# Second block with tokens on the partitions where a norm follows: one core, fp32 split into high and low parts

## What is computed

```python
def _layer_norm(x, g, b):
    mu = x.mean(-1, keepdims=True)
    var = jnp.square(x - mu).mean(-1, keepdims=True)
    return (x - mu) * lax.rsqrt(var + NORM_EPS) * g + b

for l in range(DEPTH):                       # second_block
    proj = x @ w_in[l]                       # r_q, r_k, r_v, r_g, m_qk, m_v, m_o, gates
    ...                                      # retention and mLSTM, gated and projected
    mix = (gate_a * y_ret + gate_b * y_ml) @ w_out[l]
    x = _layer_norm(DEEPNORM_ALPHA * x + mix, ln1_g[l], ln1_b[l])
    ff = (silu(x @ w_gate) * (x @ w_up)) @ w_down[l]
    x = _layer_norm(DEEPNORM_ALPHA * x + ff, ln2_g[l], ln2_b[l])
```

## Time and profile before

| | before |
|---|---|
| median of the runs | 2140.08 us |
| the profiled execution's own time | 2141.11 us |
| its span | 2139.3 us |
| PE, DVE, ACT busy | 97%, 60%, 48% |
| mean granted TensorE clock | 0.990 |

### The profile page before, as it was taken

How to read it: one execution, slowest core, us unless ns; L and a number is a source line. 1 busy time by engine, 2 the same in 40 slices (tenths; PEclk the granted TensorE clock), 3 DMA queues, 4 the chain that set the end, 5 groups by cost and what they waited for, 6 DMA issues and landing times.

```text
span 2139.3 us, 39735 instructions
## 1 busy us (share of the span) xinstructions
PE 2072.3 (97%) x16726; PEld 2017.7 (94%) x16748; DVE 1277.7 (60%) x1144; ACT 1030.1 (48%) x975; POOL 120.3 (6%) x83
## 2 busy tenths in 40 slices
PE   7999999999999998899999999999998999999997
PEld 6999998999999997699999999999998999999996
DVE  6556655655665667456557556755445666665445
ACT  5445645534443366344436454544345563545343
POOL 4000000100100002020000001010001000001001
PEclk9999999999999999899999999999999999999999
DMA  6555443455465544035545344435553443554452
GB/s 252 198 192 177 166 170 118 162 193 190 163 217 182 191 163 155 37 139 206 195 176 197 138 158 158 178 123 212 180 192 120 159 162 136 187 186 158 177 194 80
DMA packets 51562, 360.32 MB, mean 168 GB/s; under 512 B 5632, under 2 KB 7808, under 8 KB 8320
## 3 DMA queue, kind: packets, MB, share of 16 engines
q1 hardware_dynamic: 50768, 355.18, 45.8%
q0 software_dynamic: 688, 3.60, 0.5%
HBM read 357.71 MB, written 1.05 MB: 168 GB/s over the span
## 4 chain that ended last, share of the span: by engine, by line
PE 92%; DVE 4%; ACT 2%; issue 1%; POOL 0%; DMA 0%; ACTq 0%; SPq 0%; DVEq 0%; POOLq 0%
PE ps L236 25%; PE ps L237 25%; PE ps L238 25%; PE ps L283 2%; PE ps L285 2%; PE ps L284 2%; PE ps L272 1%; DVE wlo L232 1%; PE ps L267 1%; PE ps L268 1%; PE ps L585 1%; ACT whi L227 1%; PE ps L1486 1%; PE ps L1478 1%; DVE in_lo L440 1%
## 5 line engine op out<-in xcount | busy, mean ns | idle before, releaser
L232 DVE TENSOR_TENSOR wlo<-raw,whi 128x2048 fp32r<-128x2048 f32 x335 | 783.0, 2339 | 520.0 <-ACT whi L227 519.0
L236 PE MATMUL ps<-in_hi,whi 128*128 128x256 f32 x3708 | 1050.5, 283 | 10.8 <-DVE wlo L232 4.9
L237 PE MATMUL ps<-in_lo,whi 128*128 128x256 f32 x3708 | 1039.2, 280 | 0.0
L238 PE MATMUL ps<-in_hi,wlo 128*128 128x256 f32 x3708 | 1038.5, 280 | 0.0
L227 ACT ACTIVATE whi<-raw 128x2048 fp32r<-128x2048 f32 x335 | 638.4, 1908 | 238.3 <-PE ps L238 214.0
L236 PEld LDWEIGHTS ps<-in_hi,whi 128*128 128x128 f32 x3708 | 701.9, 189 | 18.6 <-issue 5.3
L237 PEld LDWEIGHTS ps<-in_lo,whi 128*128 128x128 f32 x3708 | 702.3, 189 | 2.1 <-issue 1.4
L238 PEld LDWEIGHTS ps<-in_hi,wlo 128*128 128x128 f32 x3708 | 701.9, 189 | 0.0
L236 PE MATMUL ps<-h_hi,whi 128*128 128x256 f32 x960 | 270.9, 282 | 0.0
L237 PE MATMUL ps<-h_lo,whi 128*128 128x256 f32 x960 | 269.8, 281 | 0.0
L238 PE MATMUL ps<-h_hi,wlo 128*128 128x256 f32 x960 | 269.4, 281 | 0.0
(11 more groups left out here) (251 smaller groups left out, 1728.9 us busy)
## 6 DMA issues: line engine op xcount, KB each, us to landing
raw<-in_slots SPq DMA_DIRECT2D x335, 1024.0 KB, 4.8
ws<-in_mem_t POOLq DMA_DIRECT2D x2, 1024.0 KB, 8.5
consts<-in_consts SPq DMA_DIRECT2D x1, 1600.0 KB, 13.2
consts<-in_consts POOLq DMA_DIRECT2D x1, 1472.0 KB, 6.7
x<-in_x_t SPq DMA_DIRECT2D x1, 1024.0 KB, 7.6
y_t<-x SPq DMA_DIRECT2D x1, 640.0 KB, 3.4
y_t<-x SPq DMA_DIRECT2D x1, 384.0 KB, 3.7
params<-in_params SPq DMA_DIRECT2D x1, 105.0 KB, 14.5
```

The lines of the kernel that those rows point to most:

```text
L232: dve.tensor_tensor(wlo[:, j], raw[:, j], whi[:, j].bitcast(F32), ALU.subtract).then_inc(lo_ready, 1)
L236: pe.matmul(out, whi[:, j, o:o + n], hi, start=start, stop=False, skip_group_check=True)
L237: pe.matmul(out, whi[:, j, o:o + n], lo, start=False, stop=False, skip_group_check=True)
L238: return pe.matmul(out, wlo[:, j, o:o + n], hi, start=False, stop=stop, skip_group_check=True)
```

## The change

It has these parts, all in the second block and in the FFN before it:

- The last projection before a norm (`w_out` slots, and all down slots of the last three FFNs) is multiplied with the activations as the stationary side: its result is tokens by features. A down slot is `pe_down_part` for two halves of the tokens (t) and two halves of the features (h), 24 matmuls with 512 columns of weights.
- x is kept as tokens by features (`x_tok`, two halves of 128 tokens). It is turned once, by 16 transposes in the last FFN of the first block (L547 of the new kernel), and copied back by ScalarE. The result y is stored without a turn, in three transfers.
- The norm runs along the free axis on VectorE: add, `bn_stats`, `bn_aggr`, subtract mean and multiply with the gain, multiply with 1/std and add the bias; ScalarE only takes Ln and Exp of one column. Gains and biases come as 128 equal rows by DMA (1 MB for each norm, two issues by GpSimd in each layer).
- For the next product each half is turned by 8 transposes (`pe_turn_y`) into PSUM, from which ScalarE and VectorE write `in_hi` and `in_lo`.
- The order goes by halves of the tokens: the first half of a norm's input is finished before the second, and the transposes stand inside the matmuls of the second half and of the next pair.
- The first two slots after a norm lie in an own buffer (`first_w`) instead of the ring. Their product is tokens by features; the first two slots of a layer are therefore now values (`S_RV0`), and FFN group 0 is turned back by 4 transposes (L557). The later mLSTM row product (`aT`) moves behind one slot and the retention's values.
- The layer loop is written out twice; the copy of parameters `lp` and two dummy slots at the end go.

```diff
+        x_tok = x[:, :, :].rearrange("p a b -> p (a b)").rearrange("p (t h n) -> p t h n", t=2, h=2)
...
+        def act_first_hi(act, c, u):
+            j = c % RING
+            act.wait_ge(raw_full[j], 16 * (c // RING + 1))
+            act.activation(first_hi(u), raw[:, j], ACT.Copy).then_inc(hi_ready, 1)
...
+        def turn_bank(m, t, h):
+            return ps[:, 4 + h if m % 2 else 2 * t + h, :]
+        def pe_turn_y(pe, m, t):
+            for h in range(2):
+                pe.wait_ge(y_done, 4 * m + 2 * t + h + 1)
+                for k in range(4):
+                    last = pe.transpose(turn_bank(m, t, h)[:, k * P:(k + 1) * P], x_tok[:, t, h, k * P:(k + 1) * P], ident)
+                last.then_inc(y_turned, 1)
+        def act_tok_hi(act, m, t):
+            for h in range(2):
+                act.wait_ge(y_turned, 4 * m + 2 * t + h + 1)
+                src = turn_bank(m, t, h).rearrange("p (a b) -> p a b", a=4)
+                act.activation(in_hi[:, 4 * h:4 * h + 4, t * P:(t + 1) * P], src, ACT.Copy).then_inc(tok_hi, 1)
+        def dve_tok_lo(dve, m, t):
+            for h in range(2):
+                k, a = slice(4 * h, 4 * h + 4), slice(t * P, (t + 1) * P)
+                src = turn_bank(m, t, h).rearrange("p (a b) -> p a b", a=4)
+                dve.wait_ge(tok_hi, 4 * m + 2 * t + h + 1)
+                dve.tensor_tensor(in_lo[:, k, a], src, in_hi[:, k, a].bitcast(F32), ALU.subtract).then_inc(tok_lo, 1)
...
+        def pe_tok_half(pe, out, w_hi, w_lo, t, m=None, pause=None, then=None):
+            a, o = slice(t * P, (t + 1) * P), out[:, t * 256:(t + 1) * 256]
+            for g in range(2):
+                if m is not None:
+                    pe.wait_ge(tok_hi, 4 * m + 2 * t + g + 1)
+                for k in range(4 * g, 4 * g + 4):
+                    if k == pause:
+                        then()
+                    w = slice(k * 256, k * 256 + 256)
+                    pe.matmul(o, in_hi[:, k, a], w_hi[:, w], start=(k == 0), stop=False, skip_group_check=True)
+                    pe.matmul(o, in_hi[:, k, a], w_lo[:, w], start=False, stop=False, skip_group_check=True)
+                if m is not None:
+                    pe.wait_ge(tok_lo, 4 * m + 2 * t + g + 1)
+                for k in range(4 * g, 4 * g + 4):
+                    w = slice(k * 256, k * 256 + 256)
+                    last = pe.matmul(o, in_lo[:, k, a], w_hi[:, w], start=False, stop=(k == DT - 1), skip_group_check=True)
+            return last
+        def pe_first_pair(pe, outs, m):
+            w = [(first_hi(u), first_lo(u)) for u in range(2)]
+            pe_tok_half(pe, outs[0], *w[0], 0, m)
+            pe_tok_half(pe, outs[1], *w[1], 0, None, 6, lambda: pe_turn_y(pe, m, 1))
+            pe_tok_half(pe, outs[0], *w[0], 1, m).then_inc(slot_used, 1)
+            pe_tok_half(pe, outs[1], *w[1], 1).then_inc(slot_used, 1)
...
+        def pe_down_part(pe, j, hi, lo, t, h, first=False):
+            o, a = ps[:, 2 * t + h, :], slice(t * P, (t + 1) * P)
+            for kk in range(2):
+                w = slice(kk * D + h * 512, kk * D + h * 512 + 512)
+                pe.matmul(o, hi[:, kk, a], whi[:, j, w], start=(first and kk == 0), stop=False, skip_group_check=True)
+                pe.matmul(o, hi[:, kk, a], wlo[:, j, w], start=False, stop=False, skip_group_check=True)
+                last = pe.matmul(o, lo[:, kk, a], whi[:, j, w], start=False, stop=False, skip_group_check=True)
+            return last
...
+                pe.wait_ge(fin_log, f + 1)
+                for t in range(2):
+                    for k in range(DT):
+                        last = pe.transpose(ps[:, 2 * t + k // 4, (k % 4) * P:(k % 4 + 1) * P], x[:, k, t * P:(t + 1) * P], ident)
+                last.then_inc(x_turned, 1)
+                up(0, 3, 0)
...
+                pe_first_pair(pe, (gate0_ps, up0_ps), m_in)
+                gate(0, 2, 0)
+                pe.wait_ge(ffn_mul, fb + 1)
+                for kk in range(2):
+                    for t in range(2):
+                        last = pe.transpose(ps[:, 3, kk * T + t * P:kk * T + (t + 1) * P],
+                                            hidden[:, t * 256 + kk * P:t * 256 + (kk + 1) * P], ident)
+                last.then_inc(h_turned, 1)
+                up(0, 3, 0)
+            down(0, 4, 0, True)
...
+            for h in range(2):
+                pe_down_part(pe, s9 % RING, h_hi, h_lo, 0, h)
+            pe.wait_ge(lo_ready, s10 + 1)
+            pe.wait_ge(ffn_hl, fb + LASTF + 1)
+            for h in range(2):
+                pe_down_part(pe, s10 % RING, last_hi, last_lo, 0, h).then_inc(down_half, 1)
+            for h in range(2):
+                last = pe_down_part(pe, s9 % RING, h_hi, h_lo, 1, h)
+            last.then_inc(slot_used, 1)
+            pe_down_part(pe, s10 % RING, last_hi, last_lo, 1, 0).then_inc(down_half, 1)
+            if m_out is not None:
+                pe_turn_y(pe, m_out, 0)
+            pe_down_part(pe, s10 % RING, last_hi, last_lo, 1, 1).then_inc(slot_used, 1)
...
+        gains = [view(6144, 2, 2, 512), view(8192, 2, 2, 512)]
+        def out_bank(i, t):
+            return i - 2 if i >= 2 and t else i
+        def dve_ln_add(dve, l, i, v, new, t, part):
+            dve.scalar_tensor_tensor(v, v, DEEP_ALPHA, new, ALU.mult, ALU.add).then_inc(ln_sum, 1)
+            dve.wait_ge(ln_sum, LN_SUMS * l + i)
+            dve.bn_stats(ln_parts6[:, t, 6 * part:6 * part + 6], v).then_inc(ln_stats, 1)
+        def act_ln_rstd(act, l, which, t):
+            q, r = 4 * l + 2 * which + t, ln_r[:, t:t + 1]
+            act.wait_ge(ln_mean, q + 1)
+            act.activation(r, ln_mv[:, t, 1:2], ACT.Ln, bias=eps[:, 1:2]).then_inc(ln_log, 1)
+            act.wait_ge(ln_log, q + 1)
+            act.activation(r, r, ACT.Exp, scale=-0.5).then_inc(ln_rstd, 1)
+        def dve_ln_tok(dve, l, which, t, stats, parts):
+            q = 4 * l + 2 * which + t
+            dve.wait_ge(ln_stats, LN_SUMS * l + stats)
+            dve.bn_aggr(ln_mv[:, t], ln_parts6[:, t, 0:6 * parts]).then_inc(ln_mean, 1)
+            dve.wait_ge(ln_mean, q + 1)
+            dve.wait_ge(gb_loaded[which], 16 * (l + 1))
+            g, b = gains[which][:, 0], gains[which][:, 1]
+            for h in range(2):
+                v = x_tok[:, t, h]
+                dve.scalar_tensor_tensor(v, v, ln_mv[:, t, 0:1], g[:, h], ALU.subtract, ALU.mult).then_inc(ln_centred, 1)
+            dve.wait_ge(ln_rstd, q + 1)
+            for h in range(2):
+                v = x_tok[:, t, h]
+                dve.wait_ge(ln_centred, 2 * q + h + 1)
+                dve.scalar_tensor_tensor(v, v, ln_r[:, t:t + 1], b[:, h], ALU.mult, ALU.add).then_inc(y_done, 1)
...
+        def dve_entry(dve, t, h):
+            wait_down(dve, 3, t, h)
+            dve.wait_ge(x_tok_set, 1)
+            v = x_tok[:, t, h]
+            dve.scalar_tensor_tensor(v, ps[:, 2 * t + h, :], 0.5, v, ALU.mult, ALU.add).then_inc(y_done, 1)
+        def dve_ln2_add(dve, l, t, h):
+            wait_down(dve, l + 4, t, h)
+            dve_ln_add(dve, l, 9 + 2 * t + h, x_tok[:, t, h], ps[:, 2 * t + h, :], t, h)
...
-            for i in proj(B2_OUT, 0, range(DT), parts({0: 7, 2: 8, 4: 9, 6: 10})):
-                if i:
-                    pe_ln_mean(pe, n, i - 1)
-            pe_ln_mean(pe, n, 3)
-            pe_ln_var(pe, n)
-            pe_ffn(pe, l + 4, B2_FFN, r3, ln_parts(pe, n + 1))
-            for i in range(4):
-                pe_ln_mean(pe, n + 1, i)
-            pe_ln_var(pe, n + 1)
+            c = B2_OUT + 3 * r3
+            ready = parts({0: 7, 2: 8, 4: 9, 6: 10})
+            pe.wait_ge(lo_ready, c + 1)
+            pe.matmul(ps[:, 0, :], zeros[:, 0:P], zeros[:, :], start=True, stop=False, skip_group_check=True)
...
+            out_tile(1, 0)
+            out_tile(1, 1).then_inc(slot_used, 1)
+            out_tile(2, 0).then_inc(out_half, 1)
+            out_tile(3, 0).then_inc(out_half, 1)
+            pe.wait_ge(ln_sum, LN_SUMS * l + 4)
+            out_tile(2, 1).then_inc(slot_used, 1)
+            out_tile(3, 1, 4, lambda: pe_turn_y(pe, 2 * l + 1, 0)).then_inc(slot_used, 1)
+            pe_ffn_tok(pe, l + 4, B2_FFN + 3 * r3, 2 * l + 1, 2 * l + 2 if l < LAYERS - 1 else None)
...
-            for s in range(4):
-                act_hi(act, B2_OUT + s + 2, r3)
-            act_ln_factor(act, n)
-            act_ln_parts(act, n, "ln1_b")
-            act_ln_shift(act, n, "ln1_b")
+            act_hi(act, B2_OUT + 2, r3)
+            act_hi(act, B2_OUT + 3, r3)
+            act_first_hi(act, B2_FFN + 3 * r3, 0)
+            act_first_hi(act, B2_FFN + 1 + 3 * r3, 1)
+            act_log_exp(act)
+            act_ln_rstd(act, l, 0, 0)
+            act_tok_hi(act, 2 * l + 1, 0)
+            act_hi(act, B2_FFN + 2, r3)
+            act_ln_rstd(act, l, 0, 1)
+            act_tok_hi(act, 2 * l + 1, 1)
             act_ffn(act, l + 4, B2_FFN, r3, False)
-            act_ln_factor(act, n + 1)
```

(80 more changed lines are left out.)

316 lines of the change are left out of this document (166 added, 150 removed).

## The result

The changed kernel took 2088.81 us, the median of four runs (2084.97 to 2089.54), against 2140.93 us (2138.69 to 2144.73) for the one before: ratio 0.9752, 95% interval 0.974 to 0.9763. The forecast was 2082. Three further times, on other occasions, it had 2084.71, 2088.55 and 2085.20. The profiled execution had an own time of 2088.40 us and a span of 2086.6, so 52.7 us less than the profiled one before, where the sum said 57.7.

A forecast was written before the change was run, and what follows sets the result against it. TensorE was taken to bound the kernel (busy 97%, 92% of the chain of waits). Terms 16.3 + 12.5 + 13.3 - 2.5 + 15.5 + 2.6 = 57.7 us off 2141.1, less 1.0 for the median: 2082 us, range 2073 to 2102.

The forecast's parts named there:

- the down slots: 33 slots in three FFNs: 24 matmuls of 512 columns at 0.217 us replace 48 narrow ones, 0.47 us each, 15.5 gained.
- wide matmuls bring nothing: Rival for the 512-column down matmuls: the extra 0.01 us goes with the columns, 15.5 us missing, 2098 us; chance 0.12.
- no other slot changed: Sign to look for: down slots of the last three FFNs at 5.2 us, all other slots as before.
- Norm 1: Between output projection and FFN, twice: sums and waiting go, 2.7 us cost remains, 8.2 gained per layer, 16.3 us.
- Norm 2: Between the second block's layers: 18.3 us of sums, waiting and half clock become 5.8 us, 12.5 gained.
- The end: From PE's last matmul to the end of the kernel: 22.9 us become 9.6, 13.3 us gained.
- Between the blocks: Where the first block hands to the second: 32 added transposes, 3.9 us, make a loss of 2.5 us.
- Clearing: Clearing of four banks in three FFNs goes, 12 at 0.217 us, 2.6 us gained.
- Layer 1's body: Layer 1 up to its output projection: no change, 0 us; the clock's fall inside it was taken to stay.
- no falls in the layers: Rival: two half-clock stretches inside the layers, 6.9 and 3.4 us, vanish; 5 us more gained, 2077 us; chance 0.08.
- The rival of late halves and clock: At three norms PE waits for DVE in pieces, half clock follows each: 15 us lost, 2097 us; chance 0.12.

The follow-up runs named there:

- the written-out kernel: The kernel before the change with only its second-block layer loop written out on three engines: 2135.07 us against 2139.67, ratio 0.9977.
- the narrow one: The changed kernel with each 512-column down matmul written as two of 256 columns: 2089.41 us against 2084.71 for the changed kernel.
- the one without halves: The changed kernel with the first token half's norm put behind the second half's sums: 2106.40 us, 21.7 more than the changed kernel.
- that program: A separate small program streaming independent matmuls of each format and width plus 160 transposes, only TensorE at work; 512-column fp32r took 0.227 us each.
- the split products: The changed kernel with the four fp32 selection-matrix products issued in two places of two, one slot apart: 2099.79 us against 2088.55.

## Why the prediction was right, and where it was not

The sign and the size held: the time fell within the range, 7 us above the forecast (5.0 in the profiled spans; the rest is mostly the 1.0 us taken off for the median, which this time lay 0.4 above the profiled run). The mechanism held at the norms and at the end. It did not at the down slots, the second largest term, and part of the closeness is luck.

**The step that failed is the down slots**: "I take 0.217: 5.68 - 5.21 = 0.47 us a slot, 15.5 us." The wide matmul is 0.2333 in the kernel, the slot 5.60, the gain 0.07 to 0.08 us a slot, 2.4 us. 13 us of the forecast are missing, and the rival "wide matmuls bring nothing" is the one that came true, with its 0.236. Even the 0.08 need not be the width's, since the untouched narrow slots of the first block gained as much; that also misses the forecast's "no other slot changed". The inference from fp32 to fp32r was the fault. Two fp32 records of 256 columns cost nearly what one of 512 does (0.216 and 0.429), so that row spoke for a cost that goes with the columns, and so for no gain; instead its price, which has 2 to 3 ns over the columns, was given to a format that by itself has 13 to 14, and in this kernel even those went with the columns. Even the form by itself (0.1200 and 0.2267) would have given only 0.32 us a slot. The Trainium skill ("TensorE: Matmul & The Clock Gate", Back-to-back issue gap) has N / 2.4 + 2.5 ns. Bf16 agrees (0.109 at 256), fp32r does not: 0.1167 and 0.2333 in the kernel, 0.120 and 0.227 by itself. Its estimate of the saving, 2 us, came out near the measured one through two errors that cancel.

**Why the time was still only 7 us off.** Other terms were too small by 8 us in all. Some 3 us of that hang together with the miss, since longer down slots cover more of DVE's work; that the others went the same way is luck.

- Norm 1 (16.3 us for two): 9.1 us went between the output projection and the FFN in each layer; less 0.4 for the hidden group's transposes, 17.5 in all. There is no waiting, where 0.3 us were written for each, and a transpose is 0.87 / 8 = 0.11 us, not 0.12.
- Norm 2 (12.5 us): 15.4 us went there and behind it; less 0.9 for the 8 transposes that stand in FFN 4's stage, 14.5. VectorE came as counted: from the last hidden part (1596.36) to the first y (1603.66) 7.3 us, where the count has 7.7. But PE's waits are 1.6 us and not 3.9 (none ahead of the first transposes, where 1.4 were counted), since PE arrives later: half a down slot takes 2.8 us and not 2.6, and covers DVE. Part of what the down slots did not give came back here. Some 5 us of this term are the loop's end, as the forecast said of the 3.4 us for the third slot and of the clock; the written-out kernel shows it.
- The end (13.3 us): 15.5. From the last pass of DVE (2083.43) to the end of the span are 3.2 us, where 4.1 were taken as a bound; and PE's last matmul is 0.8 us later than counted (four halves of a slot at 0.2 each), so less is left behind it.
- Between the blocks (loss 2.5): 1.9. The table's 0.8, and 1.7 that down slots and clearing gave in that stage, less 0.6 for a low part that is no longer late, which falls into layer 1.
- Clearing (2.6): 0.86 us in each FFN, as said.
- Layer 1's body, nothing in the sum: those 0.6 us, and a fall of the clock that is 3.4 us long and not 6.8, 1.7 us. The fall itself stayed, so the rival "no falls in the layers" did not come true. In layer 1 it is 3.4 us long in all four profiles of the changed kernel, and 6.8 in the kernel before, its written-out form, the narrow one and the one without halves; what sets the length no run shows.

**The rival of late halves and clock** had its premise in waits of DVE. It didn't happen since the halves hide them; the kernel without halves shows what it would have been, and more: 21.7 us, with the clock at half behind each of the three norms. It also had the rule of the Trainium skill on its side ("TensorE: Matmul & The Clock Gate", PE-mode transpose), that transposes do not count as activity. The row of 160 transposes, 17.5 us with no other work on PE, does not bear it out. Windows of that program, transposes first, then the fp32r row behind them:

```profile
185.99:203.46 17.47, 17.47 (x163) 1.00 0.00 1
203.46:214.99 11.53, 11.51 (x96) 1.00 0.01 1
```

The clock stayed at 1.00 through them and after, and so it did at the turned halves of the kernel. What the clock fell behind in the second block was waiting (norm 2 before, the three norms without halves, the slots behind the split products), and products with 4 rows in use. Waiting alone doesn't make it sure: at norm 1 of the kernel before PE stood still for 3.1 of 27 us, and the clock stayed at 1.00.

## What to carry to other kernels

When a term of the sum multiplies a small difference by many instructions, measure the form at its new size by itself before trusting it, and take it only from rows of the same number format: 16 ns on each of 792 matmuls was the largest error here. A norm between two rows of matmuls hides in halves of the tokens: the second half's matmuls cover the first half's norm, and where waiting on TensorE is followed by half the clock, as it was here behind waits of 3.7 to 4.3 us at the norms without halves, a microsecond of waiting removed is worth more than itself. Before crediting a restructuring, write out the loop alone: here 4.6 us of a gain of 51 to 55 us needed nothing else. And look at slots that weren't touched: if their price moved too, a part of the gain belongs to something else.

## What the runs showed that was not expected

- An fp32r matmul costs N / 2.4 plus 13 to 14 ns by itself (0.1205, 0.173, 0.227 us for 256, 384, 512 columns), an fp32 record twice N / 2.4 plus 2 to 3. In the FFN of the changed kernel it is 0.4557 ns a column instead (0.1167, 0.2333). The cause of the difference is open.
- The same 48 fp32r matmuls of a down slot took 5.68 us in the kernel before and 5.60 in the changed one, in code that the change left alone. The slots of the first FFN took 5.65 in two profiles of the changed kernel and 5.60 in the other two, 1.6 us in 30 slots.
- Four fp32 products in a row over 4 of 128 rows are followed by a half clock of 3.4 or 6.8 us in fourteen places of sixteen; over 128 rows, in one kernel 124 of them zero, by none in four places.
- Runs of one kernel differ by up to 7 us, and the mean granted clock goes with it: of nineteen runs of the changed kernel the fastest (2082.65 us) has 0.995 and the slowest (2089.54) 0.993. The profiles differ in how long they are at half the clock before the end, 13.7 us in the shortest and 27.3 in the longest. An effect of 2 to 3 us is read from the trace here, not from the times.
